# Attention of the third and fourth mixer: a loop over pairs of units, and each weighing behind a younger unit's transposes

## The reference

```python
# third mixer (nsa): three branches per head, each with its own gate
s = einsum('btgrd,bcgd->bgrtc', qg, kcmp) * scale          # compressed keys, 15 per group
p_cmp = softmax(where(cvalid, s, NEG_INF)); p_cmp = where(tpos >= 31, p_cmp, 0.0)
o_cmp = einsum('bgrtc,bcgd->btgrd', p_cmp, vcmp)
...                                                        # which blocks are selected
o_slc = nsa_selected_attention(qg, ks, vs, sel)            # causal softmax, keys ks, values vs
o_win = banded_attention(q, kw, vw, NSA_WINDOW)            # causal softmax, keys kw, values vw
o = g[..., 0:1] * o_cmp + g[..., 1:2] * o_slc + g[..., 2:3] * o_win

# fourth mixer (fox): causal softmax with a sum of log forget gates
s = einsum('bhqd,bkhd->bhqk', q[:, lo:hi], k[:, :hi]) * scale
s = s + c[:, :, lo:hi, None] - c[:, :, None, :hi]
p = softmax(where(causal, s, NEG_INF)); outs.append(einsum('bhqk,bkhd->bqhd', p, v[:, :hi]))
```

## Time and profile before

| | us |
|---|---|
| median of the runs | 2766.06 |
| the profiled execution, its own time | 2762.9 |
| its span in the profile | 2761.1 |
| third mixer's attention, PE's first scores to the first product of `proj_keep` | 2108.97 to 2195.53 |
| fourth mixer's attention, the same | 2494.82 to 2537.68 |
| PE busy over the span | 2678.9 (97%) |
| DVE busy | 2040.2 (74%) |
| ACT busy | 1513.7 (55%) |
| POOL busy | 612.4 (22%) |
| mean granted clock of PE | 0.991 |

### The profile page before, as it was taken

How to read it: one execution, slowest core, us unless ns; L and a number is a source line. 1 busy time by engine, 2 the same in 40 slices (tenths; PEclk the granted TensorE clock), 3 DMA queues, 4 the chain that set the end, 5 groups by cost and what they waited for, 6 DMA issues and landing times.

```text
span 2761.1 us, 60809 instructions
## 1 busy us (share of the span) xinstructions
PE 2678.9 (97%) x21671; PEld 2594.4 (94%) x21671; DVE 2040.2 (74%) x4493; ACT 1513.7 (55%) x3282; POOL 612.4 (22%) x659
## 2 busy tenths in 40 slices
PE   9999999999999999999999999999998899999998
PEld 8799989999999999899999999999987799987998
DVE  6769988787787867779987777777676666556665
ACT  6453455555555555742455555555545655556554
POOL 1034780021111214025940010000053300012000
PEclk9999999999999999999999999999998999999999
DMA  5045428787887855156257777676643056542564
GB/s 175 16 156 183 144 69 254 228 292 245 272 266 243 291 158 153 62 175 200 85 163 229 233 242 232 228 249 215 191 138 113 24 161 191 175 140 75 160 191 136
DMA packets 153654, 493.93 MB, mean 179 GB/s; under 512 B 18032, under 2 KB 37936, under 8 KB 153488
## 3 DMA queue, kind: packets, MB, share of 16 engines
q1 hardware_dynamic: 137424, 437.67, 49.2%
q0 software_dynamic: 15488, 54.11, 6.9%
q10 hardware_dynamic: 576, 0.03, 0.0%
HBM read 481.62 MB, written 10.13 MB: 178 GB/s over the span
## 4 chain that ended last, share of the span: by engine, by line
PE 85%; DVE 11%; ACT 2%; issue 1%; POOL 1%; DMA 0%; POOLq 0%; DVEq 0%; ACTq 0%
PE banks L848 68%; PE banks L1092 5%; PE banks L1113 2%; PE banks L990 2%; DVE meta_row L2381 1%; DVE work L2384 1%; PE banks L886 1%; PE banks L1254 1%; PE banks L881 1%; DVE w_lo L552 1%; POOL x_lo L2887 1%; DVE arena L2323 1%; ACT w_hi L545 1%; DVE arena L2270 1%; DVE arena L2263 1%
## 5 line engine op out<-in xcount | busy, mean ns | idle before, releaser
L552 DVE TENSOR_TENSOR w_lo<-ring,w_hi 128x512 fp32r<-128x512 f32 x1448 | 1015.1, 704 | 516.3 <-ACT w_hi L545 487.0
L545 ACT ACTIVATE w_hi<-ring 128x512 fp32r<-128x512 f32 x1448 | 909.3, 630 | 716.9 <-PE banks L848 694.8
L848 PE MATMUL banks<-gated_all,w_hi 128*128 128x240 f32 (+1 forms) x5120 | 877.3, 275 | 6.6 <-DVE gated_all L2448 6.6
L848 PE MATMUL banks<-x_hi,w_hi 128*128 128x240 f32 (+2 forms) x2752 | 773.0, 281 | 11.2 <-POOL x_lo L2887 7.9
L848 PEld LDWEIGHTS banks<-gated_all,w_hi 128*128 128x128 f32 x5120 | 772.1, 189 | 8.5 <-DVE gated_all L2448 8.5
L848 PE MATMUL banks<-x_hi,w_lo 128*128 128x240 f32 (+2 forms) x2752 | 766.1, 278 | 0.0
L848 PE MATMUL banks<-x_lo,w_hi 128*128 128x240 f32 (+2 forms) x2752 | 765.0, 278 | 0.0
L848 PE MATMUL banks<-gated_all,w_lo 128*128 128x240 f32 (+1 forms) x2560 | 705.6, 276 | 0.0
L848 PEld LDWEIGHTS banks<-x_hi,w_hi 128*128 128x128 f32 x2752 | 522.5, 190 | 22.2 <-issue 10.1
L848 PEld LDWEIGHTS banks<-x_hi,w_lo 128*128 128x128 f32 x2752 | 522.1, 190 | 0.0
L848 PEld LDWEIGHTS banks<-x_lo,w_hi 128*128 128x128 f32 x2752 | 521.6, 190 | 0.4
(11 more groups left out here) (386 smaller groups left out, 3225.9 us busy)
## 6 DMA issues: line engine op xcount, KB each, us to landing
ring<-in_peer_v SPq DMA_DIRECT2D x256, 512.0 KB, 3.6
ring<-in_peer_u SPq DMA_DIRECT2D x184, 512.0 KB, 4.6
arena<-in_peer_u SPq DMA_DIRECT2D x72, 512.0 KB, 3.6
ring<-in_mlp_up SPq DMA_DIRECT2D x64, 512.0 KB, 4.0
ring<-in_mlp_down SPq DMA_DIRECT2D x64, 512.0 KB, 3.9
ring<-w_peer_query SPq DMA_DIRECT2D x32, 512.0 KB, 3.5
ring<-w_fox_proj SPq DMA_DIRECT2D x24, 512.0 KB, 3.5
ring<-w_nsa_proj SPq DMA_DIRECT2D x20, 512.0 KB, 3.5
```

What stands on the lines that cost most here:

```text
L545: act.activation(w_hi[:, hn % SPLITS], raw_half(hn), ACT.Copy).then_inc(hi_ready, 1)
L552: dve.tensor_tensor(w_lo[:, hn % SPLITS], raw_half(hn), w_hi[:, hn % SPLITS].bitcast(F32), ALU.subtract)\
L848: mm = pe.matmul(out, w_at(w), x, start=start and j == 0, stop=stop and j == 2, skip_group_check=True)
```

## The change

- All three engines loop over pairs, j from 0. PE in a pass: `scores(2j + 2)`, `turn(2j - 2)`, `weigh(2j - 4)`, `turn(2j - 1)`, `weigh(2j - 3)`. Before, the two weighings of this pass were of units 2j - 3 and 2j - 2.
- ACT in a pass: both exponentials of pair j, then both roundings of pair j - 1. DVE: maxima of pair j, scaling of pair j - 1, both remainders of pair j - 2.
- The maxima come out negated from the reduction, with no product and no join. SCALE moves into the queries: ACT's copy gets it as its scale and DVE's subtraction becomes a `scalar_tensor_tensor` in `fox_proj`; in `nsa_proj` ACT's copy ahead of the rotation gets it. The exponentials lose their scale, and the forget sums are no longer divided by it.
- In the last pair of each stage DVE scales the wide rows too, and POOL's loop ends two units earlier.
- In the third mixer: the compressed branch's products come behind the units' own in chunk 0 (unit 5), others as before; PE waits for its weights at unit 4, not 3. Its scores and their turn come directly behind the second pair of scores, with six `keep_warm` products ahead. On DVE the values' split moves behind the shift and the weighing of the compressed map, the keys' split right behind the spread of the values. On ACT an exponential of one column, whose only use is to load the table, and the key copy stand ahead of the first exponentials.

```diff
+                pairs = len(units) // 2
+                scores(0)
+                if not fox:
+                    compress_turn(1)
+                    compress_out()
+                for j in range(pairs + 2):
+                    if j == 0 and fox:
                         pe.wait_ge(v_split, 3 * NT)
+                    if j + 1 < pairs:
+                        scores(2 * (j + 1))
+                    if j == 0 and not fox:
+                        keep_warm(WARM_FILL, 3)
+                        cmp_scores()
+                        cmp_scores_turn()
+                    if j == 0 and fox:
                         keep_warm(WARM_FILL, 5)
...
+                    for u in (2 * j, 2 * j + 1):
+                        if 1 <= j <= pairs:
+                            turn(u - 2)
+                        if j >= 2:
+                            weigh(u - 4)
+                    if j == 3 and not fox:
                         cmp_turn()
...
                 def turn(u):
                     pe.wait_ge(pair_scaled, p0 + u + 1)
-                    pe.wait_ge(pair_scaled_pool, p0 + u + 1)
+                    if u < len(units) - 2:
+                        pe.wait_ge(pair_scaled_pool, s["u0"] + u + 1)
...
+                pairs = len(units) // 2
+                for j in range(pairs + 2):
+                    if j == 0 and not fox:
+                        act.activation(lam_exp[:, 0:1], eps, ACT.Exp)
+                        keep_cmp_keys()
+                    if j < pairs:
+                        exps(2 * j)
+                        exps(2 * j + 1)
+                    if j == 0 and not fox:
+                        keep_cmp_scores()
+                    for u in (2 * j - 2, 2 * j - 1):
+                        if 0 <= u < len(units):
+                            round_turned(u)
+                    if j == 1 and not fox:
+                        cmp_exps()
+                    if j == 2 and not fox:
+                        keep_cmp_values()
+                    if j == 3 and not fox:
                         cmp_round()
...
                     for t in range(NT):
-                        steps.mark(dve.reduce_max(pair_row_max[:, both, t], banks[:, score_bank(u):score_bank(u) + 2, score_cols(t)], AX_X))
-                    steps.join()
-                    dve.tensor_scalar(pair_neg_max[:, both], pair_row_max[:, both], -SCALE, None, ALU.mult).then_inc(pair_max, 2)
+                        ins = dve.tensor_reduce(pair_neg_max[:, both, t], banks[:, score_bank(u):score_bank(u) + 2, score_cols(t)], AX_X,
+                                                ALU.max, negate=True)
+                    ins.then_inc(pair_max, 2)
...
                     for i in range(2):
-                        dve.tensor_scalar(pair_p[:, u % 4 + i, 0:P], pair_p[:, u % 4 + i, 0:P], cf[:, i, 0:1], None, ALU.mult)\
-                           .then_inc(pair_scaled, 1)
+                        for t, n in enumerate((P, SEQ) if u + 2 == len(units) else (P,)):
+                            row = pair_p[:, u % 4 + i, t * SEQ:t * SEQ + n]
+                            ins = dve.tensor_scalar(row, row, cf[:, i, t:t + 1], None, ALU.mult)
+                        ins.then_inc(pair_scaled, 1)
...
+                pairs = len(units) // 2
+                for j in range(pairs + 3):
+                    if j < pairs:
+                        maxima(2 * j)
+                    if j == 0 and not fox:
                         widen_cmp_values()
                         split_cmp_keys()
+                    if 1 <= j <= pairs:
+                        scale_rows(2 * j - 2)
+                    if j == 1 and not fox:
+                        cmp_shift()
+                    if j == 4 and not fox:
+                        cmp_rest()
+                    for u in (2 * j - 4, 2 * j - 3):
+                        if 0 <= u < len(units):
+                            turned_rest(u)
+                    if j == 2 and not fox:
                         cmp_weigh()
+                    if j == 3 and not fox:
                         split_cmp_values()
...
-                    dve.tensor_tensor(lo, banks[:, m % 4, 0:SEQ], hi.bitcast(F32), ALU.subtract).then_inc(bank_free, 1)
+                    dve.scalar_tensor_tensor(out=lo, in0=banks[:, m % 4, 0:SEQ], scalar=SCALE if m < NC else 1.0, in1=hi.bitcast(F32),
+                                             op0=ALU.mult, op1=ALU.subtract).then_inc(bank_free, 1)
...
-                for u in range(len(units)):
+                for u in range(len(units) - 2):
                     pool.wait_ge(pair_coef, s["p0"] + u + 1)
```

More of the change, by code:

```diff
@@ L700, in pair_units, with final_unit @@
             return units
+        def final_unit(units, c):
+            last = next(u for u, un in enumerate(units) if un["chunk"] == c and un["last"])
+            return 5 if last == 3 and len(units) > 2 * NC else last
         def block_rows(eng, kv):
@@ L1394, in weigh @@
                     first = un["first"]
[L1395 to L1400 removed]
+                    if not fox and u == 4:
+                        pe.wait_ge(cmp_pT_ready, 1)
+                    if not fox and un["last"] and u != 3:
+                        weigh_cmp(un["chunk"], False)
                     for kt, (vh, vl) in enumerate(un["v"]):
@@ L1404, in weigh, with weigh_cmp @@
                         for n, (v, p) in enumerate(((vh, ph), (vh, pl), (vl, ph))):
-                            mm = pe.matmul(o, v, p, start=first, stop=un["last"] and kt == 1 and n == 2, skip_group_check=True)
+                            mm = pe.matmul(o, v, p, start=first, stop=un["last"] and kt == 1 and n == 2 and (fox or u != 3),
+                                           skip_group_check=True)
                             first = False
+                    if not fox and u == 5:
+                        mm = weigh_cmp(0, True)
                     mm.then_inc(pair_weighed, 1)
+                def weigh_cmp(c, stop):
+                    pair, r = c // 4, c % 4
+                    for n, (v, p) in enumerate(((vc_hi, cmp_pT_hi), (vc_hi, cmp_pT_lo), (vc_lo, cmp_pT_hi))):
+                        mm = pe.matmul(banks[:, 4 + c % 2, 0:SEQ], v[:, pair, r], p[:, pair], start=False, stop=stop and n == 2,
+                                       skip_group_check=True)
+                    return mm
                 if fox:
@@ L2073, in fox_proj @@
                     dst = q_hi[:, m] if m < 8 else k_hi[:, m - 8]
-                    act.activation(dst, banks[:, m % 4, 0:SEQ], ACT.Copy).then_inc(qk_hi, 1)
+                    act.activation(dst, banks[:, m % 4, 0:SEQ], ACT.Copy, scale=SCALE if m < NC else 1.0).then_inc(qk_hi, 1)
                 act.wait_ge(forget_parts, 1)
```

95 lines of the change are left out of this document (23 added, 72 removed).

## The result

The changed kernel takes 2749.78 us (median of 20 runs, 2740.45 to 2766.49) against 2765.59 (20 runs, 2758.71 to 2775.86). The ratio is 0.9943, 95% interval 0.9928 to 0.9959: faster by 0.57%. The forecast was 2752.6, in a range of 2744 to 2760. The profiled execution took 2745.82 us, 17.1 less than that of before; its span is 2744.0.

The account below looks back on a forecast made before the run. A ring of waits, not a full engine, bounds the third mixer's attention. Terms 1.9 + 8.8 - 0.3 + 1.3 + 1.9 - 0.1 = 13.5 us off the median 2766.06 give 2752.6, range 2744 to 2760.

Parts of the forecast that it names:

- The ring: Third mixer's attention: waits through PE, ACT, DVE and POOL set a pass of 4.41 us; fourth mixer 4.17.
- steady terms: Savings of 8.8 us over ten passes in the third mixer and 1.9 over four in the fourth.
- What is late next: Third mixer's pass once the ring is cut: PE 3.53 us, DVE 3.24, the remaining chain 2.9; PE bounds.
- Rival 1: DVE or its handovers become the bound at about 3.95 us a pass; saving about 7, total 2759; chance 0.14.
- Rival 3: The ring isn't cut and the waits return one place later at the same period; 2766 us; chance 0.06.
- Rival 4: PE stays at 1.2 GHz in the steady loop, so the kernel gets slower; 2787.9 us; chance 0.03.
- The ramp of the third mixer: Start of the third mixer's attention: turn 6 at 2137.4 instead of 2139.31, 1.9 us gained, between nothing and 3.5.
- Rival 2: TensorE's clock is kept up in the ramp: up to 5.2 us more, down to 2747.4; chance 0.09.
- The page's rule: Third mixer's ramp: the clock drop behind PE's 4.07 us idle goes, making the sum 15.1 instead of 13.5.
- The ramp of the fourth: Start of the fourth mixer's attention: the first weighing's 0.84 us wait and that pass's stall go, 1.3 us gained.
- The tails: Ends of both attentions, wide rows on DVE: losses of 0.3 us (third) and 0.1 (fourth).
- Negated maxima: DVE's pass: products and join removed, 0.19 us together; negation adds at most 0.17 each pass, costing nothing under PE.

Follow-up runs that it names:

- e4: The changed kernel with plain maxima, a join and a product by -1 instead of negated maxima; ratio to the kernel before 0.9924.
- after again: The changed kernel, unedited, in another execution; ratio to the kernel before 0.9924, third mixer's attention 76.13 us.
- after: The first profiled execution of the changed kernel, unedited; it took 2745.82 us, third mixer's attention 71.51 us.
- e6: The changed kernel with more warming matmuls in the third mixer and at the start of the fourth's attention; ratio to the kernel before 0.9937.

## Why the prediction was right, and where it was not

- **The ring** was what bound a pass, and its period could be read from POOL's idle and busy time. Confirmed: with the remainder still ahead of the maxima and PE's order changed, the period follows the lengthened ring (5.16), and with all of the change it is PE's own work, 3.53 forecast and 3.53 measured, 3.70 and 3.69 to 3.70 in the fourth mixer. The steady terms were 8.8 and 1.9; they measured 9.08 and 1.93. The 0.3 more comes from the kernel before, whose ten passes took 44.39: nine of 4.40 to 4.41 and one of 4.76.
- **What is late next.** PE, then DVE close behind. DVE measured (3.11 + 3.88 - 0.41) / 2 = 3.29 a pass against 3.24 forecast. Rival 1 (3.95 a pass, DVE or its handovers; by its own period it would have cost 5 us of the 13.5, not the half that it says) didn't come; even with the product back, e4, DVE stays under PE. Rival 3 falls with POOL's idle of 1.58 (1.6 forecast; 1.8 and 1.78 in the fourth). Rival 4 falls with a clock of 1.00 over the steady part.
- **The ramp of the third mixer** is the term that was mis-sized: 1.9, measured 5.36 in one execution and 0.75 in another. The step that failed is what the prediction says of the clock: "The forecast keeps the slow start and counts nothing for the later drop." Neither half held in every execution.
  - *Up to the shift* I had "2124.04 - 1.4 = 2122.6", 13.6 us into the stage. With the early fall, as in the trace that I read it from, it is 13.3, so that the forecast was right; without it, it is 10.2. In both DVE stands idle ahead of the shift (2.26 and 4.31 us). What sets its place is when PE has turned the compressed scores, and DVE's values' split is not what mattered. The prediction says that the clock fell twice in the ramp, but it shows only one fall; the other, 0.51 over 2112.57 to 2119.57 in the same trace, is the larger, and has no price of its own.
  - *From the shift to turn 6* I had 14.8, measured 14.81 where the clock is 1.00 over 20 to 27.5 us, with the weighting at 2.14 (2.2) and the values' split at 1.20 (1.4). A compressed remainder of 0.60 that I had left out made up for what these and the passes took less. Where the clock falls there (0.77) it is 16.3: in after again DVE waits ahead of that very remainder. DVE's timeline, first of after, then of after again:

```profile
2119.89 0.88 DVE L2675 TENSOR_TENSOR arena<-banks,arena 128x256 f32<-128x256 f32 x2 [2.26 <-PE banks L1354]
```

```profile
2125.33 0.89 DVE L2675 TENSOR_TENSOR arena<-banks,arena 128x256 f32<-128x256 f32 x2 [4.31 <-PE banks L1354]
...
2140.33 0.69 DVE L2693 TENSOR_TENSOR cmp_pT_lo<-banks,cmp_pT_hi 128x512 fp32r<-128x512 f32 x1 [1.39 <-ACT cmp_pT_hi L2003]
```

- **Rival 2** (the clock kept up, up to 5.2 more, 2747.4) is what partly happened in the profiled execution. It isn't something the change does each time. The forecast's 2752.6 and the rival's 2747.4 lie on both sides of the 2749.78 measured, and the executions of the changed kernel show both kinds of start. That the total came so near owes something to luck: how often each kind comes in unprofiled executions isn't known.
- **The page's rule**, that TensorE should not be left idle for long between bursts (the Trainium skill, "TensorE: Matmul & The Clock Gate", "Why this matters for your kernels"), was to add 1.6 us if the fall behind the 4.07 us idle went. The trace doesn't bear out this use of it: the 4.07 is gone, and a fall stays in the ramp (0.66 at 15 to 20 us) behind waits of 0.69 and 1.96 us. In the fourth mixer e6 agrees with the rule: the 2.69 us idle are cut to 0.61 and the fall is gone.
- **The ramp of the fourth**: 1.3, measured 1.61 (2.67 in the second execution, where the clock is at half for a shorter time, 9.84 instead of 10.91 us until turn 0).
- **The tails**: -0.3 and -0.1, measured +0.61 and +0.03. The gain is one more pass of the loop, which my tails left out: turn 26 to turn 28 takes 3.25 us instead of 4.40, and turn 10 to turn 12 of the fourth 3.06 instead of 4.17. Behind the last pair's turns the stages do lose, more than the 0.3 and 0.1: from turn 30 to the end it is 4.62 us instead of 3.89, from turn 14 of the fourth 4.32 instead of 3.54. The four scalings on DVE took 0.93 from start to next start; I had put the wide ones at 0.28 to 0.56 each, and 0.62 of the 0.93 had been there before. So they cost 0.3 together. One by one the trace has 0.20 for each narrow and 0.26 for each wide one; in the other pairs, with POOL's scaling beside them, the two narrow ones take 0.20 and 0.42. So part of what the wide ones cost comes back from the narrow ones. The turn of unit 30 waits 0.75 now, 0.88 before.
- **Negated maxima**: a reduction with negate takes 1.00 to 1.01 for two, as the plain ones. From the maxima's start to the reciprocal's it is 1.01 to 1.07 instead of 1.20. Nothing in the steady part (e4), as forecast; about 1 us in the ramp, where the prediction has 3.04 for a pass, measured 2.96 (the prediction put the negated maxima into that sum at the plain ones' time).
- **SCALE in the projections**: nothing, as forecast. The three-operand form costs the same as the subtraction, 418 ns against 418; the bound of 0.9 us was needless. DVE by line there:

```profile
L2810 DVE SCALAR_TENSOR_TENSOR q_lo<-banks,q_hi 128x256 fp32r<-128x256 f32 x8 | 3.3, 418 | 0.0
```

- The wait for the compressed weights moved the turn by nothing: no idle stands ahead of the weighing behind turn 6 in after (2134.70, weighing at 2134.98).

In the profiled execution the total was 17.1, not 13.5: the ramps gained 3.8 more than forecast, the steady parts 0.3 and the tails 1.0, and 1.5 us went outside the two stages. The mechanism, the cut ring, is what the steady parts show; their 10.7 forecast and 11.0 measured don't depend on the clock's falls.

## What to carry to other kernels

Where three in-order engines pass work in a ring, write down the order of each as a list, and follow the ring back from an engine with a constant idle time; the period is that idle time plus its work. This change had to move every engine's order together: each half of it alone made a pass longer (5.16 and 4.78 against 4.41). And read the granted clock in windows of a few us over the whole start of a stage, in two executions where one can, before a difference there is put down to the code.

## What the runs showed of the hardware

- The same kernel with the same waits on PE has its clock at half for 7 us in some executions and not in others (0.54 and 1.00 over the same 7 us), which delays the shift by 3.1 us. In all three executions that had this fall in the changed order the later one at 20 to 27.5 us came too, 4.6 us together of 2750.
- The same fall costs nothing or 1.5 us, as it meets a stretch in which PE waits or one in which it is the bound.
- A scaling of 128x256 float32 values on DVE took 0.26 us from start to next start, one of 128x128 0.20, in the last pair of the third mixer, where POOL does nothing; on POOL one of 128x256 takes 0.96. Of two narrow ones beside POOL's scaling the second took 0.42, in the kernel before and in the changed one. That POOL is the cause isn't shown by an experiment of its own.
